# Two stacked blocks on one core: where the head shares, their spreads and the stick weights' meetings stand in a hand-written order

## The chip, the cores and the metric

One core of a Trainium2 chip runs the whole program. The metric is the device time of one execution in microseconds; the kernel before took 3168.99 us, the median of three runs (3164.33 to 3171.9). The engines are named as in the profile: PE is TensorE, DVE VectorE, ACT ScalarE, POOL GpSimd, SP the queue that issues most transfers.

## The reference

A first block of two layers, then a second block of one layer, all float32, on 1024 tokens of width 1024.

```python
def first_block(...):                      # two layers
    for i in range(DEPTH):
        hn = rmsnorm(h, norm1[i])
        z = hn @ w_in[i]
        ...
        pool_out = pool_mixer(u, pool_w[i], pool_scale[i])
        attn_out = dilated_mixer(q, k, v)
        h = h + jnp.concatenate([pool_out, attn_out], axis=-1) @ w_out[i]
        hn = rmsnorm(h, norm2[i])
        h = h + jnp.square(jax.nn.relu(hn @ w_up[i])) @ w_down[i]
        gate = jax.nn.sigmoid(rmsnorm(h, norm3[i]) @ w_gate[i])
        h = h + gate * (p[i] @ w_ple[i])
    return rmsnorm(h, final_norm)
```

The dilated mixer has 12 heads in three groups (patterns) of four. Each group attends in its own windows; a softmax over the three groups' log-sums gives each group a share for every token and head, and the group's output is scaled by it:

```python
    wts = jax.nn.softmax(jnp.stack(lses, axis=0), axis=0)
    o = jnp.concatenate([outs[g] * wts[g][..., None] for g in range(len(DIL_PATTERNS))], axis=2)
```

The second block has eight heads of stick-breaking attention beside a causal convolution of 31 taps:

```python
        causal = s_pos < t_pos
        log_fail = jnp.where(causal, jax.nn.log_sigmoid(-z), 0.0)
        later = lax.cumsum(log_fail, axis=3, reverse=True) - log_fail
        w = jnp.where(causal, jnp.exp(jax.nn.log_sigmoid(z) + later), 0.0)
        outs.append(jnp.einsum('bhts,bshd->bthd', w.astype(vb.dtype), vb))
```

## The kernel before, in words

Every large product is made in three matmuls per piece of the contraction (high and low parts of both operands). A **half** is one output panel of 128 features by 512 tokens: eight **chunks** in the projections (three matmuls of 512 columns each), five in part A of the output product and three in part B. The halves of a layer are numbered m = 2 * panel + token half. Two PSUM banks take the halves of the projections and of parts A and B in turn (`half_bank_no`), so half m + 2 cannot start before DVE has taken half m.

All smaller work is placed between chunks by a table: `weave` (L198) puts jobs at (m, k), that is behind chunk k of half m; `put_a` does the same for part A, counting chunks from its start, five to a half. Each engine goes through the same table. PE does a job's matmuls behind the chunk named. DVE and ACT, however, go through all jobs of half m in the order of k and then take half m (DVE `woven` and `take_qk`, `take_v`, `add_to`; ACT `woven`). So a job's place on DVE is ahead of the take of its half, and a waiting job holds back all behind it.

The jobs at stake in the first block, done for two sets of heads (c = 0 and 1) in each of two layers:

- `step`: attention of one unit (one pattern, two heads). ACT writes each unit's statistics to DRAM (L1891 to L1897), and SP reads the three patterns of a set back (`read_stats`, L878, waited for as `stats_in`).
- `shares`: on DVE `share_weights` (L2352 to L2374) clears `rows` in set 0, waits for the read-back and makes the softmax over groups in eight small steps; ACT gives the exponential (L1915). PE has nothing to do in it.
- `turn_w`: PE turns the weights (L1387) into the one side bank, ACT copies the high part (L1920), DVE makes the low part (L2379, `lower_rows`).
- `spread`: PE spreads a group's rows over its features (L1395) into the side bank, DVE multiplies the attention output by them (L2387), ACT makes the high part (L1924), DVE the low part (L2389); the last two are `weigh`. Each needs the side bank free of the job before it (`side_starts`, L1288).

In set 0 the jobs lie in the halves 28 to 33, eight chunks each, with attention steps of unit 3 between them; in set 1 in part A, halves 48 to 53.

The second block's attention goes over four pairs of heads (c = 0 to 3) and 12 rounds each, placed every fourth chunk as a step u (`weave2`, L330). One step does, on PE, `turn_weights` of round u - 2 (L1615, waits for DVE's product `z_weighed`, L2718), after groups of rounds are complete a `meet` with the values (L1602; groups 0 to 3 at u = 4, 6, 10 and 14, of 8, 16, 24 and 32 matmuls in the profile's count) and `score` of round u (L1628). ACT makes two sigmoids of the scores (L2116, L2117), DVE scans (L2711, L2713) and multiplies (L2718), POOL masks and also splits the weights of the panels (L1168, L1171). The steps 12 to 14 of a pair lie in steps 0 to 2 of the next (`step_parts`). Pair 3 runs in the halves of Z_ATT, where DVE has the gates to take as well.

Of the kernel before, what the change touches and what calls it, by code (L numbers as in the profile page):

```python
# [197 lines left out]
def weave():  # L198
    at = {}

    def put(m, k, *job):
        at.setdefault(m, []).append((k, job))

    def put_a(u, *job):
        put(2 * PART_A + u // len(CHUNKS_A), u % len(CHUNKS_A), *job)

    put(3, 4, "stat", 0)
    put(5, 4, "stat", 1)
    for hf in range(2):
        put(UP_AT[hf], 7, "stat2", hf)  # L210
        put(GATE_AT + 2 * hf, 7, "stat3", hf)
        for c in range(2):
            put(late_at(1 + 2 * hf, c), 2, "turn_p", c, hf)
    for unit in range(UNITS - 1):
        m0 = 2 * (2 + 3 * (unit + 1))
        put(m0, 1, "turn_v", unit, 0)
        put(m0, 4, "turn_v", unit, 1)
        for i in range(STOPS):
            k = 11 + 10 * i
            put(m0 + k // KC, k % KC, "step", unit, i)  # L220
    for c in range(2):
        for hf in range(2):
            put(26 + c, 0 + 4 * hf, "pool", c, hf)
    put(28, 3, "stat_in", 0)
    put(29, 4, "shares", 0)
    for hf in range(2):
        put(30 + 2 * hf, 0, "turn_w", 0, hf)
        put(30 + 2 * hf, 4, "spread", 0, hf, 0)
        put(31 + 2 * hf, 0, "spread", 0, hf, 1)
        put(31 + 2 * hf, 4, "spread", 0, hf, 2)  # L230
    put_a(1, "turn_v", 5, 0)
    put_a(4, "turn_v", 5, 1)
    for i in range(STOPS + LAG):
        put_a(8 + 7 * i, "step", 5, i)
    put_a(36, "stat_in", 1)
    put_a(41, "shares", 1)
    for hf in range(2):
        put_a(45 + 10 * hf, "turn_w", 1, hf)
        for g in range(GROUPS):
            put_a(48 + 10 * hf + 2 * g, "spread", 1, hf, g)  # L240
    for m in at:
        at[m].sort(key=lambda x: x[0])
    return at
# [67 lines left out]
PAIRS = 4  # L311
# [13 lines left out]
ROUNDS = [(qb, part, min(HALF, P * (qb + 1) - HALF * part)) for qb in range(8) for part in range(1 + qb // 4)]  # L325
# [26 lines left out]
def step_parts(c, u):  # L352

    return ((c - 1, u + len(ROUNDS)), (c, u)) if c and u < MEET_LAG else ((c, u),)
# [9 lines left out]
def meets_after(u):  # L364

    r = u - MEET_LAG
    if 0 <= r and ROUNDS[r][0] % 2 and (r + 1 == len(ROUNDS) or ROUNDS[r + 1][0] != ROUNDS[r][0]):
        return ROUNDS[r][0] // 2
    return None
# [38 lines left out]
def two_blocks(nc, x, p, positions, norm1, w_in, pool_w, pool_scale, w_out, norm2, w_up, w_down,  # L408
# [848 lines left out]
    def _(pe):  # L1257
# [332 lines left out]
        def meet(c, g):  # L1590


            group = 4 * c + g
            r = max(i for i, (qb, part, n) in enumerate(ROUNDS) if qb == 2 * g + 1)
            pe.wait_ge(z_taken, 2 * (len(ROUNDS) * c + r + 1))
            if group:
                pe.wait_ge(att_taken, group)
            for kb in range(7, 5 - 2 * g, -1):
                at = max(0, 7 - kb - 2 * g) * P
                for e in range(2):  # L1600
                    rows = slice(64 * e, 64 * e + 64)
                    mm = t.matmul(meet_bank[rows, at:256], v2[c % 2][:, kb, rows], weight_t[:, kb, e, at:256],  # L1602
                                  start=(kb == 7), stop=True, skip_group_check=True)
            mm.then_inc(z_met, 1)

        def turn_weights(c, r):
            nth, blocks = len(ROUNDS) * c + r, ROUNDS[r][2] // P
            pe.wait_ge(z_weighed, nth + 1)
            if r == 0:
                pe.wait_ge(v2_taken, 2 * c + 2)  # L1610
            for e in range(2):
                if nth:
                    pe.wait_ge(z_taken, 2 * (nth - 1) + e + 1)
                for i in range(blocks):
                    mm = t.transpose(turn_banks[e][:, i * P:i * P + P], weight[:, nth % 2, e, i * P:i * P + P], ident[:])  # L1615
                mm.then_inc(z_turned, 1)
# [14 lines left out]
        def woven2(m2, k):  # L1631
            for at, job in WEAVE2.get(m2, ()):
                if at != k:
                    continue
                kind, args = job[0], job[1:]
                if kind == "stat":
                    sum_features(DEPTH, args[0], sum_no(DEPTH - 1, Y_HN1, 7, args[0]) + 1, *job)
                elif kind == "turn_v2":
                    turn_v2(*args)
                else:  # L1640
                    for c, u in step_parts(*args):
                        if TURN_LAG <= u < len(ROUNDS) + TURN_LAG:
                            turn_weights(c, u - TURN_LAG)
                    for c, u in step_parts(*args):
                        if meets_after(u) is not None:
                            meet(c, meets_after(u))
                    for c, u in step_parts(*args):
                        if u < len(ROUNDS):
                            score(c, u)

# [1264 lines left out]
```

## Time and profile before

| | |
|---|---|
| median of 3 runs | 3168.99 us (3164.33, 3168.99, 3171.9) |
| profiled execution, its time | 3167.66 us |
| profiled execution, its span | 3165.9 us |
| PE busy | 3121.7 us, 99% |
| DVE busy | 2045.6 us, 65% |
| POOL busy | 1713.6 us, 54% |
| ACT busy | 977.1 us, 31% |
| granted TensorE clock, mean | 0.996 |

The span runs from the first to the last instruction; the execution's own time has 1.8 us more around it. Busy PE is not PE at its peak: a matmul counts while it runs, at whatever clock was granted. A line of the views reads: start, duration, engine and line of the kernel, what it writes and reads, and in brackets how long the engine had been idle and what released it.

### The profile page before, as it was taken

How to read it: one execution, taken by the hardware profiler on the slowest of the kernel's cores; microseconds unless marked ns; L12 is line 12 of the kernel's file. 1: busy time of each engine (PE TensorE's matmuls, PEld its weight loads, DVE VectorE, ACT ScalarE, POOL GpSimd, SP SyncE). 2: the span in 40 equal slices, each digit the busy share in tenths (PEclk: the TensorE clock that was granted, in tenths of full speed). 3: DMA queues.
4: the chain of work that ended last, by engine and by line, in shares of the span. 5: the costliest groups of instructions: out<-in, count | busy, mean ns of one | idle time of the engine just before them, and what ended most of it. 6: DMA issues, size and time to landing. Idle time of an engine off the chain costs nothing.

```text
span 3165.9 us, 39438 instructions
## 1 busy us (share of the span) xinstructions
PE 3121.7 (99%) x14756; PEld 2518.2 (80%) x14756; DVE 2045.6 (65%) x2749; ACT 977.1 (31%) x1847; POOL 1713.6 (54%) x1544
## 2 busy tenths in 40 slices
PE   8999999999999999999999999999999999999999
PEld 6777788888888888777788888888888776688887
DVE  6656476666665664555676666664768988798323
ACT  3222253333332421222343333332432244402112
POOL 5632355666566546522465666565445533376574
PEclk9999999999999999999999999999999999999999
DMA  5211211111112122112131111112111100011112
GB/s 155 55 40 37 81 57 54 54 52 49 56 54 67 45 94 62 40 41 86 39 57 54 54 48 53 55 54 66 46 47 47 34 27 27 21 50 47 50 54 87
DMA packets 306349, 173.73 MB, mean 55 GB/s; under 512 B 61424, under 2 KB 296944, under 8 KB 306160
## 3 DMA queue, kind: packets, MB, share of 16 engines
q1 hardware_dynamic: 287904, 162.55, 17.7%
q10 hardware_dynamic: 18256, 8.67, 0.9%
q8 instruction: 118, 1.93, 0.2%
q14 instruction: 71, 0.58, 0.1%
HBM read 155.13 MB, written 12.91 MB: 53 GB/s over the span
## 4 chain that ended last, share of the span: by engine, by line
PE 91%; DVE 7%; issue 1%; ACT 1%; DMA 0%; ACTq 0%; DVEq 0%; SPq 0%
PE ring L1261 17%; PE ring L1263 16%; PE ring L1262 16%; PE aux L1261 5%; PE aux L1263 5%; PE aux L1262 5%; PE ring L1523 3%; PE ring L1522 3%; PE ring L1521 3%; PE aux L1523 2%; PE aux L1522 2%; PE aux L1521 2%; DVE conv_out L2670 1%; PE aux L1341 1%; PE aux L1358 1%; PE aux L1602 1%
## 5 line engine op out<-in xcount | busy, mean ns | idle before, releaser
L1010 POOL TENSOR_TENSOR w_hi<-w_raw,ones 128x512 fp32r<-128x512 f32 (+3 forms) x408 | 449.9, 1103 | 894.2 <-PE ring L1263 712.3
L1013 POOL TENSOR_TENSOR w_lo<-w_raw,w_hi 128x512 fp32r<-128x512 f32 (+3 forms) x408 | 533.9, 1308 | 32.0
L1261 PE MATMUL ring<-Q_hi,w_hi 128*128 128x512 f32 x1312 | 519.1, 396 | 0.0
L1263 PE MATMUL ring<-Q_hi,w_lo 128*128 128x512 f32 x1312 | 511.3, 390 | 0.0
L1262 PE MATMUL ring<-Q_lo,w_hi 128*128 128x512 f32 x1312 | 510.9, 389 | 0.0
L1261 PEld LDWEIGHTS ring<-Q_hi,w_hi 128*128 128x128 f32 x1312 | 246.2, 188 | 76.3 <-issue 26.4
L1263 PEld LDWEIGHTS ring<-Q_hi,w_lo 128*128 128x128 f32 x1312 | 246.3, 188 | 52.3
L1262 PEld LDWEIGHTS ring<-Q_lo,w_hi 128*128 128x128 f32 x1312 | 246.4, 188 | 50.4 <-issue 1.0
L1261 PE MATMUL ring<-P_hi,w_hi 128*128 128x512 f32 x656 | 271.0, 413 | 3.0 <-DVE pool_u L2288 1.3
L1262 PE MATMUL ring<-P_lo,w_hi 128*128 128x512 f32 x656 | 258.2, 394 | 0.0
L1263 PE MATMUL ring<-P_hi,w_lo 128*128 128x512 f32 x656 | 258.0, 393 | 0.0
L1261 PE MATMUL aux<-Q_hi,w_hi 128*128 128x512 f32 x544 | 213.2, 392 | 0.0
L1263 PE MATMUL aux<-Q_hi,w_lo 128*128 128x512 f32 x544 | 211.7, 389 | 0.0
L1262 PE MATMUL aux<-Q_lo,w_hi 128*128 128x512 f32 x544 | 211.7, 389 | 0.0
L1974 ACT ACTIVATE aux<-tmp 128x512 f32<-128x512 f32 x112 | 67.4, 602 | 403.2 <-DVE tmp L2435 403.2
L2670 DVE SCALAR_TENSOR_TENSOR conv_out<-conv_in,taps,conv_out 128x1021 f32<-128x1021 f32 (+29 forms) x120 | 185.7, 1594 | 0.2
L1261 PEld LDWEIGHTS ring<-P_hi,w_hi 128*128 128x128 f32 x656 | 124.8, 190 | 42.7 <-issue 14.3
L1263 PEld LDWEIGHTS ring<-P_hi,w_lo 128*128 128x128 f32 x656 | 124.4, 190 | 27.3
L1262 PEld LDWEIGHTS ring<-P_lo,w_hi 128*128 128x128 f32 x656 | 124.6, 190 | 25.9 <-issue 2.9
L1037 POOL TENSOR_TENSOR w_lo<-w_sums,w_hi 128x1024 fp32r<-128x1024 f32 x56 | 134.5, 2401 | 0.0
L1025 POOL TENSOR_TENSOR w_sums<-w_raw 128x256 f32<-128x256 f32 x56 | 41.4, 739 | 159.5 <-issue 152.7
L1261 PEld LDWEIGHTS aux<-Q_hi,w_hi 128*128 128x128 f32 x544 | 102.1, 188 | 22.1 <-DVE Q_lo L2252 0.8
(400 smaller groups left out, 7043.1 us busy)
## 6 DMA issues: line engine op xcount, KB each, us to landing
w_raw<-in_w_in SPq DMA_DIRECT2D x84, 512.0 KB, 3.8
w_raw<-in_w_up SPq DMA_DIRECT2D x64, 512.0 KB, 4.0
w_raw<-in_w_down SPq DMA_DIRECT2D x64, 512.0 KB, 3.4
h_scratch<-h ACTq DMA_DIRECT2D x16, 512.0 KB, 3.7
w_raw<-in_w_gate SPq DMA_DIRECT2D x16, 512.0 KB, 4.0
hx<-h_scratch SPq DMA_DIRECT2D x12, 512.0 KB, 7.8
x_raw<-in_x SPq DMA_DIRECT2D x8, 512.0 KB, 7.7
w_raw<-in_w_out SPq DMA_DIRECT2D x16, 256.0 KB, 2.8
```

Of the source, the lines that this page charges most:

```text
L1010: g.tensor_tensor(w_hi[:, slot, ks], w_raw[:, slot, ks], one.broadcast_to([P, width, P]), ALU.mult).then_inc(w_hi_ready, 1)
L1013: g.tensor_tensor(w_lo[:, slot, ks], w_raw[:, slot, ks], w_hi[:, slot, ks].bitcast(F32), ALU.subtract).then_inc(w_ready, 1)
L1025: g.tensor_tensor(s1, a21, a22, ALU.add).then_inc(s_made, 1)
L1037: g.tensor_tensor(w_lo[:, slot], w_sums[:, slot], w_hi[:, slot].bitcast(F32), ALU.subtract).then_inc(w_ready, 1)
L1261: t.matmul(o, wh, xh, start=first, stop=False)
L1262: t.matmul(o, wh, xl, start=False, stop=False)
L1263: return t.matmul(o, wl, xh, start=False, stop=last)
L1521: t.matmul(to[at], wh, xh, start=(i == 0 and not joins), stop=False, skip_group_check=True)
L1522: t.matmul(to[at], wh, xl, start=False, stop=False, skip_group_check=True)
L1523: mm = t.matmul(to[at], wl, xh, start=False, stop=(i == 1), skip_group_check=True)
L1974: a.activation(square_bank, tmp[:], ACT.Square).then_inc(squared, 1)
L2670: v.scalar_tensor_tensor(conv_out[:, c, shift:], conv_in[:, c, 0:S - shift], tap, conv_out[:, c, shift:], ALU.mult, ALU.add)\
```

## The change

Three edits. In `weave` the job `shares` of set 0 goes from (29, 4) to (28, 6). The turnings and spreads of set 1 go from part A's chunks 45, 48, 50, 52 and 55, 58, 60, 62 to 45, 49, 52, 55 and 59, 63, 66, 69. In PE's `woven2` the meeting of a stick step goes ahead of its turning, except for groups 0 and 1 of the pairs 0 to 2; where a step serves two pairs, all of the earlier pair's work now goes ahead of all of the next one's.

```diff
--- before.py
+++ after.py
@@ -222,7 +222,7 @@
         for hf in range(2):
             put(26 + c, 0 + 4 * hf, "pool", c, hf)
     put(28, 3, "stat_in", 0)
-    put(29, 4, "shares", 0)
+    put(28, 6, "shares", 0)
     for hf in range(2):
         put(30 + 2 * hf, 0, "turn_w", 0, hf)
         put(30 + 2 * hf, 4, "spread", 0, hf, 0)
@@ -235,9 +235,9 @@
     put_a(36, "stat_in", 1)
     put_a(41, "shares", 1)
     for hf in range(2):
-        put_a(45 + 10 * hf, "turn_w", 1, hf)
+        put_a(45 + 14 * hf, "turn_w", 1, hf)
         for g in range(GROUPS):
-            put_a(48 + 10 * hf + 2 * g, "spread", 1, hf, g)
+            put_a(49 + 14 * hf + 3 * g, "spread", 1, hf, g)
     for m in at:
         at[m].sort(key=lambda x: x[0])
     return at
@@ -1639,12 +1639,15 @@
                     turn_v2(*args)
                 else:
                     for c, u in step_parts(*args):
-                        if TURN_LAG <= u < len(ROUNDS) + TURN_LAG:
+                        group = meets_after(u)
+                        turns = TURN_LAG <= u < len(ROUNDS) + TURN_LAG
+                        early = group is not None and group < 2 and c < PAIRS - 1
+                        if turns and early:
                             turn_weights(c, u - TURN_LAG)
-                    for c, u in step_parts(*args):
-                        if meets_after(u) is not None:
-                            meet(c, meets_after(u))
-                    for c, u in step_parts(*args):
+                        if group is not None:
+                            meet(c, group)
+                        if turns and not early:
+                            turn_weights(c, u - TURN_LAG)
                         if u < len(ROUNDS):
                             score(c, u)
 
```

Below the third edit all line numbers are three higher. The order of DVE in layer 0, set 0, from the last attention statistics of half 29 on, before:

```order
L2343 TENSOR_SCALAR neg_max<-row_stat 128x2
L2358 MEMSET rows 128x512
L2360 TENSOR_TENSOR top<-read_back 128x16
L2362 TENSOR_TENSOR top<-top,read_back 128x16
L2364 TENSOR_TENSOR share<-read_back,top 128x48
L2366 TENSOR_TENSOR shared_sum<-share,read_back 128x48
L2368 TENSOR_TENSOR total<-shared_sum 128x16
L2370 TENSOR_TENSOR total<-total,shared_sum 128x16
L2372 RECIPROCAL total<-total 128x16
L2374 TENSOR_TENSOR weights<-share,total 128x48
L2308 TENSOR_TENSOR q_t_82<-ring,rope_c 128x4x128
L2299 TENSOR_TENSOR q_t_82<-q_t_82,swapped_rows 128x4x128
```

And in the changed kernel, from the last operation ahead of half 28's take on (L2361 is L2358 of before, and so on):

```order
L2302 TENSOR_TENSOR k_t_85<-k_t_85,swapped_rows 128x512
L2361 MEMSET rows 128x512
L2363 TENSOR_TENSOR top<-read_back 128x16
L2365 TENSOR_TENSOR top<-top,read_back 128x16
L2367 TENSOR_TENSOR share<-read_back,top 128x48
L2369 TENSOR_TENSOR shared_sum<-share,read_back 128x48
L2371 TENSOR_TENSOR total<-shared_sum 128x16
L2373 TENSOR_TENSOR total<-total,shared_sum 128x16
L2375 RECIPROCAL total<-total 128x16
L2377 TENSOR_TENSOR weights<-share,total 128x48
L2311 TENSOR_TENSOR q_t_82<-ring,rope_c 128x4x128
L2315 TENSOR_TENSOR s_half<-ring,rope_s 128x512
```

The share chain (MEMSET to `weights`) stood behind the attention step of half 29 and ahead of that half's take; it now stands ahead of the take of half 28 (`q_t<-ring,rope_c`), with the step behind it.

PE at step 6 of pair 3, where `ident,weight` is the turning, `weight_t,v` the meeting and `k,q` the score (+ is the changed kernel):

```order
 L1262 MATMUL ring<-Q_lo,w_hi 128x512
 L1263 MATMUL ring<-Q_hi,w_lo 128x512
+L1602 MATMUL aux<-weight_t,v_1_159 64x256 x6
+L1602 MATMUL aux<-weight_t,v_1_159 64x128 x2
 L1615 MATMUL aux<-ident,weight 128x128 x4
 L1615 MATMUL ring<-ident,weight 128x128 x4
-L1602 MATMUL aux<-weight_t,v_1_159 64x256 x6
-L1602 MATMUL aux<-weight_t,v_1_159 64x128 x2
```

The 8 matmuls of the meeting went ahead of the turning; the score stays behind both.

PE in part A of layer 0, behind the first turning of set 1 (`rows,sel` is a spread, the others are chunks of the output product):

```order
 L1262 MATMUL ring<-shared_lo_97,w_hi 128x512
 L1263 MATMUL ring<-shared_hi_95,w_lo 128x512
+L1261 MATMUL ring<-pool_hi,w_hi 128x512
+L1262 MATMUL ring<-pool_lo,w_hi 128x512
+L1263 MATMUL ring<-pool_hi,w_lo 128x512
 L1395 MATMUL ring<-rows,sel 128x512
 L1261 MATMUL ring<-pool_hi,w_hi 128x512
 L1262 MATMUL ring<-pool_lo,w_hi 128x512
 L1263 MATMUL ring<-pool_hi,w_lo 128x512
-L1261 MATMUL ring<-pool_hi,w_hi 128x512
-L1262 MATMUL ring<-pool_lo,w_hi 128x512
-L1263 MATMUL ring<-pool_hi,w_lo 128x512
```

The first spread went one chunk back, the second is two chunks on, outside this piece.

## Rows read from the trace of the kernel before

**Rows 1.** The page, busy time of each engine, its share and instructions.
```profile
PE 3121.7 (99%) x14756; PEld 2518.2 (80%) x14756; DVE 2045.6 (65%) x2749; ACT 977.1 (31%) x1847; POOL 1713.6 (54%) x1544
```

**Rows 2.** Waits of PE, whole span: us in total, times, longest.
```profile
PE ring L1387 <- DVE weights L2374: 8.8, 2, 4.4
...
PE aux L1615 <- DVE weight L2718: 5.6, 4, 2.0
...
PE ring L1395 <- DVE attn L2387: 2.0, 4, 0.5
```

**Rows 3.** Stretches: us, busy time (and instructions) by engine, PEclk, DMA share, GB/s.
```profile
237.22:241.80 4.58, 4.58 (x13) 3.53 (x14) 3.09 (x4) 0.59 (x1) 0.00 (x0) 0.51 0.04 7
...
2704.92:2710.30 5.38, 5.38 (x28) 3.02 (x29) 4.42 (x7) 1.21 (x3) 0.00 (x0) 0.68 0.12 35
```

**Rows 4.** Timeline of PE, halves 30 to 32: start, us, engine, line, operation, [idle <-releaser].
```profile
237.22 1.01 PE L1387 MATMUL ring<-ident,weights 128*6 128x128 f32 x4 [4.40 <-DVE weights L2374]
...
242.50 0.39 PE L1395 MATMUL ring<-rows,sel 128*128 128x512 f32 x1
...
257.26 0.60 PE L1387 MATMUL ring<-ident,weights 128*6 128x128 f32 x4
...
262.52 0.47 PE L1395 MATMUL ring<-rows,sel 128*128 128x512 f32 x1 [1.88 <-DVE rows L2379]
```

**Rows 5.** Timeline of DVE, halves 28 to 30 of layer 0.
```profile
224.62 1.05 DVE L2308 TENSOR_TENSOR q_t<-ring,rope_c 128x512 f32<-128x512 f32 x1 [4.71 <-PE ring L1263]
225.59 0.69 DVE L2312 TENSOR_TENSOR s_half<-ring,rope_s 128x512 f32<-128x512 f32 x1
...
231.04 0.48 DVE L2358 MEMSET rows<- 128x512 f32 x1
...
236.99 1.05 DVE L2308 TENSOR_TENSOR q_t<-ring,rope_c 128x512 f32<-128x512 f32 x1
...
239.66 0.68 DVE L2379 TENSOR_TENSOR rows<-ring,rows 6x512 fp32r<-6x512 f32 x1
```

**Rows 6.** Read-back of statistics, layer 0: the SP queue's timeline, then its landing.
```profile
218.90 0.37 SPq L878 DMA_DIRECT2D read_back<-stats_scratch  x1
...
read_back<-stats_scratch SPq DMA_DIRECT2D x1, 48.0 KB, 4.2
```

**Rows 7.** Timeline of DVE, the share chain of set 1.
```profile
357.95 0.36 DVE L2360 TENSOR_TENSOR top<-read_back 128x16 f32<-128x16 f32 x1
...
361.34 0.21 DVE L2374 TENSOR_TENSOR weights<-share,total 128x48 f32<-128x48 f32 x1
```

**Rows 8.** Timelines of PE and DVE, spreads of set 1.
```profile
368.42 0.50 PE L1395 MATMUL ring<-rows,sel 128*128 128x512 f32 x1 [0.51 <-DVE attn L2387]
...
365.07 0.69 DVE L2387 TENSOR_TENSOR attn<-ring,attn 128x512 f32<-128x512 f32 x1 [1.07 <-PE ring L1395]
...
367.09 0.68 DVE L2545 TENSOR_TENSOR hx<-ring,hx 128x512 f32<-128x512 f32 x1
```

**Rows 9.** Timeline of PE, stick of pair 3.
```profile
2704.92 0.66 PE L1615 MATMUL aux<-ident,weight 128*128 128x128 f32 x4 [2.02 <-DVE weight L2718]
...
2728.15 0.66 PE L1615 MATMUL aux<-ident,weight 128*128 128x128 f32 x4 [1.91 <-DVE weight L2718]
...
2744.78 0.65 PE L1615 MATMUL aux<-ident,weight 128*128 128x128 f32 x4 [0.70 <-DVE weight L2718]
```

**Rows 10.** The chain that ended last: start, us, what.
```profile
2514.45 1.67 PE aux L1602 x16
...
2706.01 3.05 PE aux L1602 x16
```

**Rows 11.** Timeline of DVE, stick of pair 3.
```profile
2711.48 2.50 DVE L2713 TENSOR_TENSOR_SCAN left<-fail,not_yet 128x512 f32<-128x512 f32 x2 [1.79 <-ACT fail L2116]
...
2734.14 2.50 DVE L2713 TENSOR_TENSOR_SCAN left<-fail,not_yet 128x512 f32<-128x512 f32 x2 [0.81 <-ACT fail L2116]
...
2738.60 4.21 DVE L2711 TENSOR_TENSOR_SCAN left<-fail,left 128x511 f32<-128x511 f32 x2 [0.60 <-ACT fail L2116]
```

## The prediction

> **What bounds the kernel now.** The busy times come first: the matmul engine (PE) works 3121.7 of 3165.9 us [rows 1], so only its idle time and the time that it spends at a lower clock can be won, and no edit here removes a matmul. The view of waits then says who holds PE up [rows 2]. Three of its lines touch the change: the turning of the shares waits for the vector engine (DVE), 2 times, 8.8 us in all; the turning of the stick weights waits for DVE, 4 times, 5.6 us; the spreads of the second set wait for the product that reads the side bank before them, 4 times, 2.0 us. That is 16.4 us. The stretches show a second price: after the wait at 237.22 the granted clock is 0.51 for 4.58 us, after the one at 2704.92 it is 0.68 over 5.38 us [rows 3], so part of each runs at 1.2 and not at 2.4 GHz. Last, the engines' own rows give the order at each place [rows 4 to 11].
>
> **Shares of the first set.** PE puts the turning of half 30 behind its first chunk and waits 4.40 us, to 237.22 [rows 4]. DVE is late because its share job stands in the list behind the attention step of half 29: it starts with the clearing of rows at 231.04, and behind it come the take of half 29 at 236.99 and the low rows at 239.66 [rows 5]. The change puts the same nine instructions ahead of the take of half 28. DVE sat idle 4.71 us before that take, from 219.91 to 224.62 [rows 5]; the clearing fits there at no cost. The rest needs the statistics read back. That transfer is issued at 218.90 and takes 4.2 us, so it is there at 223.1 [rows 6]. The chain then costs between 3.60 us, as in the second set (357.95 to 361.55) [rows 7], and some 6 us as here, where it shares its time with GpSimd (231.04 to 236.99) [rows 5]. I take the first, since it is the same chain away from the attention step, and end at 226.7, at most 229.1. Queued behind it is the take of half 28, 1.7 us (224.62, then 225.59 for 0.69) [rows 5]: it ends at 228.4 to 230.8 instead of 226.3. Its bank is wanted by PE at the start of half 30, near 232, so nobody waits; the swaps that the SP queue issues behind this take, and the weight load behind them, go up to some 4 us later, and their readers come a half or more afterwards. The turning, due at 237.22 - 4.40 = 232.82, finds its weights made. What is late next? The spread four chunks on. From the take of half 29 to the end of the low rows DVE needs 3.35 us (236.99 to 240.34) [rows 5]; the take can now start at about 232.2, when its half is done, so they end at 235.6. From turning to spread PE needs 3.38 us at full clock: in the second half 257.26 to 262.52 less the 1.88 us of waiting [rows 4]. The spread is due at 236.2, so no wait comes back. Besides, the 5.28 us from 237.22 to 242.50 [rows 4] shrink to 3.38, which is 1.90 us of clock. Sum per layer 4.40 + 1.90 = 6.30, in two layers **12.6 us**. Upper bound: all that the stretch lost, 4.58 x 0.49 = 2.24, gives 13.3. Lower bound: a wait of 1.88, as the second half of this set has at the same place [rows 4], takes the place of the old one: 12.6 - 3.8 = 8.8.
>
> [...]
>
> **Spreads of the second set.** The third spread of each half waits 0.51 us [rows 8]: two chunks after the one before is too soon. A chunk is about 0.7 us: the 3.38 us above less the turning's 0.60, by four [rows 4]. One more covers the wait: 4 x 0.51 = 2.04 us gained. The last spread now stands behind the end of half 53, and both it and the one before fall into the same DVE list, ahead of the take of that half. A weighing takes DVE 2.02 us (365.07 to 367.09) and the take 0.68 [rows 8]; with the spread's 0.50 this is 3.2 us for one, and about 3.6 when the previous weighing is still in the way, against the next half's five chunks, 3.5 us, until PE wants the bank again. So there may be a new wait per layer, of nothing up to the 0.51 that these spreads waited so far; I take 0.2. Sum **1.6 us**, between 1.0 and 2.0.
>
> **Stick.** In pair 3 every meeting is now ahead of the turning; in the other pairs that of group 2 is, and that of group 3 goes ahead of the next pair's first turning. Of the four waits only one lies in another pair, at a meeting of group 1 whose order stays, so the other pairs give nothing. In pair 3 the turning of step 6 waits 2.02 us and that of step 10 waits 1.91 [rows 9]. The meeting behind them does not need the new weights: 16 matmuls are 1.67 us at full clock, but 3.05 after the 2.02 us wait [rows 10]. Put ahead, it hides 1.67 of 2.02 us, and with 0.35 us idle the clock should hold, so the score comes about 3.4 us earlier. But PE then waits for DVE again: the last turning, step 13, waits 0.70 us already [rows 9]. So PE gains there what DVE gains, and DVE can only lose its own idle time, that spent on scores: 1.79 + 0.81 + 0.60 = 3.20 us [rows 11]. I take **3.2 us**. Bounds: one scan pair more or fewer beside GpSimd, 4.21 against 2.50 us [rows 11], gives 1.5 or 4.9.
>
> **Sum.** 12.6 + 1.6 + 3.2 = 17.4 us. Against the profiled execution (3167.66 us) that gives 3150.3; the median of the runs shown, 3168.99, stands 1.3 us higher, so I forecast **3151.6 us**. With all low bounds 11.3 us (3157.7), with all high ones 20.2 us (3148.8).
>
> **Rivals.**
> - The first set's wait moves to its spread (the low bound above): 8.8 + 1.6 + 3.2 = 13.6, 3155.4 us. For it: DVE shows exactly this in the second half. Against: there a step stands directly before, here none does. 12%.
> - The stick gives nothing: with the scores earlier, GpSimd's weight splits fall on DVE's scans, the wait at step 13 grows above 2 us and the clock falls there, at 5.38 x 0.32 = 1.7 us [rows 3]. 12.6 + 1.6 - 1.7 = 12.5, 3156.5 us. Against: DVE's 3.20 us of idle time are real. 8%.
> - The fall of the clock near 2706 is not due to the wait and stays or moves: 1.7 us less, 15.7, 3153.3 us. For it: waits of 1.88 and 1.91 us have no such fall near them. 4%. [...]
> - Slower: the read-back is late. DVE now waits in order for it ahead of the take of half 28, and PE needs that bank near 232. With chain and take of 5.3 to 7.7 us behind the landing, PE waits once the landing passes 224.3 to 226.7; measured is 223.1 [rows 6]. Each microsecond beyond costs one per layer. To lose 6.3 us net it would have to come 23.7 / 2 = 11.9 us past that point: about 3175 us. 2%.
> - The change does too little to see: the waits return at the next instruction. 3166 us. 4%.
>
> **Numbers.** The forecast as worked out has the remaining 70%. A measurement of this kernel tells apart about 0.2%, 6.3 us; the three runs shown spread over 7.6 us. The range is 3147 to 3158.5: the bounds of the sum, the first three rivals, and 1 to 2 us of scatter; it leaves out the last two rivals. Faster 0.94, same 0.04, slower 0.02.
>
> **What would show it.** The shares' turning has no line among the waits and the granted clock is full after it, in both layers; the share chain on DVE starts near 220 and resumes at the landing; the second half's wait of 1.88 us is still there. The third spreads show no wait; a small one may appear at the start of half 55. In pair 3 step 6 waits about 0.35 us, step 10 nothing, step 13 up to 1.5 us, and the stretch from step 6 to the last meeting is 3 to 4 us shorter. I am wrong if a wait of over 1 us appears before the spread of half 30 or at the start of half 30, or if the stick keeps its length.

## The result, and the profile after

The changed kernel takes **3148.39 us**, median of 4 runs (3147.88 to 3148.72), against 3167.69 us for the kernel before in the same measurement (4 runs, 3164.33 to 3171.9): ratio 0.9935, 95% interval 0.9923 to 0.9947. Forecast were 3151.6 us, with a range of 3147 to 3158.5. The gain is 19.3 us where 17.4 were worked out. Of the 3.2 us between forecast and time, 1.3 are the base: the forecast was counted from 3168.99 us, and the kernel before has 3167.69 here. Timed once more beside the experiments, the changed kernel gave 3148.39 us again (5 runs), and the kernel before 3168.95 (9 runs).

The page of the changed kernel, its busy times, which answer to [rows 1]:

```profile
span 3146.5 us, 39438 instructions
...
PE 3116.4 (99%) x14756; PEld 2515.3 (80%) x14756; DVE 2038.8 (65%) x2749; ACT 978.4 (31%) x1847; POOL 1717.0 (55%) x1544
```

PE is busy for 5.3 us less with the same instructions. Most of that is clock; some of it is only in the counting, since a matmul's row ahead of a wait is counted 0.16 us longer than its place in a steady row (shown under e2). The rest of the gain is idle time.

The view of waits of PE over the whole span, which answers to [rows 2] (columns: waited for, us in total, times, longest):

```profile
PE ring L1395 <- DVE rows L2382: 3.7, 2, 1.9
...
PE aux L1615 <- DVE weight L2721: 2.2, 3, 1.7
...
PE ring L1317 <- DVE v_feat L2324: 0.5, 2, 0.3
```

The lines for the turning of the shares (8.8 us) and for the spreads behind the product that reads the bank (2.0 us) are gone. The stick's line fell from 5.6 to 2.2 us. The second half's wait for the low rows, 1.88 us in each layer, stands as before [rows 4]; it is now the largest that this part of the program has left.

DVE's timeline in the first set of layer 0, which answers to [rows 5]:

```profile
220.19 0.48 DVE L2361 MEMSET rows<- 128x512 f32 x1
222.83 0.85 DVE L2363 TENSOR_TENSOR top<-read_back 128x16 f32<-128x16 f32 x1 [2.16 <-DMA read_back<-stats_scratch]
...
225.40 0.21 DVE L2377 TENSOR_TENSOR weights<-share,total 128x48 f32<-128x48 f32 x1
225.52 1.05 DVE L2311 TENSOR_TENSOR q_t<-ring,rope_c 128x512 f32<-128x512 f32 x1
...
232.40 1.07 DVE L2311 TENSOR_TENSOR q_t<-ring,rope_c 128x512 f32<-128x512 f32 x1 [1.18 <-PE ring L1263]
...
235.12 0.68 DVE L2382 TENSOR_TENSOR rows<-ring,rows 6x512 fp32r<-6x512 f32 x1
```

The clearing runs where the prediction put it, then DVE waits 2.16 us for the read-back, and the chain is over at 225.61, 2.8 us after it resumed. The take of half 28 begins 0.90 us later than before (225.52 against 224.62 [rows 5]; 0.23 of that is the longer start of this execution), that of half 29 waits for PE as it should, and the low rows end at 235.80.

PE's timeline at the same place, which answers to [rows 4]:

```profile
232.88 0.60 PE L1387 MATMUL ring<-ident,weights 128*6 128x128 f32 x4
...
236.07 0.40 PE L1395 MATMUL ring<-rows,sel 128*128 128x512 f32 x1
...
256.08 0.47 PE L1395 MATMUL ring<-rows,sel 128*128 128x512 f32 x1 [1.88 <-DVE rows L2382]
```

No wait stands at the turning or at the first spread. Between the low rows' end (235.80) and the spread (236.07) lie 0.27 us: it was closer than the prediction's 0.6.

The stretches of PE (columns: window, its length, busy time and instructions of PE, PEld, DVE, ACT and POOL, then granted clock, DMA share, GB/s): from the turning to the first spread in both layers, then from the second half's spread to the next in layer 1 and in layer 0:

```profile
232.88:236.07 3.19, 3.19 (x17) 2.62 (x16) 2.88 (x4) 0.59 (x1) 3.11 (x3) 1.00 0.03 8
1391.85:1395.04 3.19, 3.19 (x18) 2.62 (x16) 2.88 (x4) 0.59 (x1) 3.11 (x3) 1.00 0.00 0
...
1415.04:1419.69 4.65, 4.65 (x13) 3.69 (x14) 1.81 (x3) 0.63 (x1) 0.00 (x0) 0.63 0.42 111
256.08:259.12 3.04, 3.04 (x14) 2.52 (x14) 1.80 (x3) 0.63 (x1) 0.00 (x0) 1.00 0.12 22
```

Before, the stretch behind the turning ran at 0.51 of full clock in layer 0 [rows 3] and at 0.52 in layer 1 (1404.65 to 1409.23); both run at the full 2.4 GHz now. The third is new: behind the 1.86 us wait of layer 1 a part of the stretch is at 1.2 GHz, and 1.6 us of the gain are given back there. The same wait in layer 0 has no such fall.

PE's timeline in the stick, pair 3, which answers to [rows 9]:

```profile
2687.81 1.04 PE L1602 MATMUL aux<-weight_t,v 128*64 128x256 f32 x10
2689.08 0.66 PE L1615 MATMUL aux<-ident,weight 128*128 128x128 f32 x4 [0.23 <-DVE weight L2721]
...
2698.27 0.66 PE L1615 MATMUL aux<-ident,weight 128*128 128x128 f32 x4 [0.28 <-DVE weight L2721]
...
2707.58 2.60 PE L1602 MATMUL aux<-weight_t,v 128*64 128x256 f32 x24
2710.29 0.66 PE L1615 MATMUL aux<-ident,weight 128*128 128x128 f32 x4
```

The first row shows the last 10 of the meeting's 16 matmuls. The meeting comes first and the turning waits only 0.23 us at step 6 and next to nothing at step 10; the 0.28 us at 2698.27 is the turning of step 8, which has no meeting beside it. Where the time is bound now is shown by the chain that ended last, from step 10 to step 13 (start, us, what):

```profile
2710.47 1.93 DVE left L2714 x2
...
2719.53 3.92 DVE left L2714 x2
2723.57 1.79 DVE weight L2721
2725.41 0.66 PE aux L1615 x4
```

It runs along DVE's scans and weighings, and PE waits 1.72 us at step 13 (0.70 before [rows 9]). DVE's timeline, at the three places where it had been idle for 1.79, 0.81 and 0.60 us before [rows 11]:

```profile
2693.76 2.54 DVE L2716 TENSOR_TENSOR_SCAN left<-fail,not_yet 128x512 f32<-128x512 f32 x2
...
2715.61 2.33 DVE L2716 TENSOR_TENSOR_SCAN left<-fail,not_yet 128x512 f32<-128x512 f32 x2
...
2719.53 3.91 DVE L2714 TENSOR_TENSOR_SCAN left<-fail,left 128x511 f32<-128x511 f32 x2 [0.23 <-DVE weight L2721]
```

No idle time is left but the 0.23 us behind each weighing, which stood before too. From the scan ahead of step 6 to the end of the last weighing DVE takes 41.91 us where it took 45.44: 3.5 us less, 3.2 of them idle time.

### The span cut at four landmarks

Every kernel below, the experiments' too, can be cut at four starts on PE: the first pooling turn of layer 0, that of layer 1, the first score of the stick and its last meeting. These are lengths in us, each from one profiled execution, worked out from starts in PE's timeline. "Rest" runs to the end of the span.

```
kernel                        start   layer 0  layer 1    stick    rest
before                       201.16   1167.76  1117.13   265.71  414.14
changed                      201.39   1159.27  1110.32   261.40  414.15
changed, once more           201.49   1159.22  1110.40   261.39  414.15
e1 shares only               198.98   1161.10  1110.55   267.70  414.16
e2 spreads only              201.46   1166.31  1114.65   266.53  414.15
e3 meetings only             200.25   1167.13  1116.67   261.39  414.14
e4 meeting first everywhere  202.55   1159.19  1110.29   262.11  414.15
e5 meetings, pair 3 only     200.56   1167.43  1116.60   262.85  414.14
e6 shares at (29, 2)         200.75   1159.52  1108.77   261.39  414.15
e7 late spread               199.29   1158.73  1108.16   261.37  414.15
e8 late end of stick         200.14   1159.19  1110.73   261.59  412.14
e9 e7 and e8                 201.23   1158.96  1108.61   261.60  412.09
e11 e9 and late turns of v   202.07   1157.36  1106.85   261.57  412.08
```

Changed against before: 8.49 in layer 0, 6.81 in layer 1, 4.31 in the stick, less 0.23 in the start and 0.01 in the rest, 19.37 us; the spans differ by 19.4. The start varies by 3.6 us between kernels that are alike in it, so small gains are read from the other columns and not from a single span. The start holds differences that no edit touches: they are not explained here.

### The profile page after: what moved, and what is told of

Its sections match the earlier page's. It is cut to its first block, busy times and chain, and to the rows that moved or that the text cites. A ratio compares the mean times of both kernels' runs of the same rounds, so it can differ in the third digit from the quotient of the medians.

```text
span 3146.5 us, 39438 instructions
## 1 busy us (share of the span) xinstructions
PE 3116.4 (99%) x14756; PEld 2515.3 (80%) x14756; DVE 2038.8 (65%) x2749; ACT 978.4 (31%) x1847; POOL 1717.0 (55%) x1544
## 4 chain that ended last, share of the span: by engine, by line
PE 94%; DVE 4%; issue 1%; ACT 1%; DMA 0%; ACTq 0%; DVEq 0%; SPq 0%
PE ring L1261 17%; PE ring L1263 17%; PE ring L1262 17%; PE aux L1261 5%; PE aux L1263 5%; PE aux L1262 5%; PE ring L1523 3%; PE ring L1521 3%; PE ring L1522 3%; PE aux L1521 2%; PE aux L1523 2%; PE aux L1522 2%; PE aux L1341 1%; PE aux L1358 1%; PE aux L1628 1%; PE aux L1602 1%
```

## The experiments

### Each part alone

**e1_shares**, the kernel before with the first edit only:

```
-    put(29, 4, "shares", 0)
+    put(28, 6, "shares", 0)
```

> Kernel before with one part of the change: the set-0 shares at (28, 6) instead of (29, 4). Theory 1 (the waits at the first spread of set 0 are the price of a share chain that starts too late, in both layers): both waits go, the first spread of layer 0 comes about 6.4 to 6.7 us earlier and that of layer 1 as much again, so 12.6 to 13.3 us off in all, about 3154.5 to 3155.5. The 1.88 us wait of the second half's spread stays in both layers; in the profile of the change it had a clock fall behind it in layer 1 only. If that fall (about 1.6 us) comes here too, the gain reads some 1.6 us smaller. Rival (the gain of the change in set 0 exists only beside the other two edits): under 10 us, with a new wait at or before half 30.

Measured: 3153.09 us median (3150.37 to 3158.54, 4 runs) against 3168.55 (19 runs), ratio 0.9952, interval 0.9937 to 0.9967. Layer 0 is 6.66 us shorter and layer 1 is 6.58, **13.2 us** in all, at the top of what theory 1 expected; the rival is out. (The medians differ by 15.5 us, but this kernel's four runs lie 8.2 us apart, and the columns are one execution each.) No clock fall stands behind the 1.90 us wait of either layer here. The view of waits holds no line for the turning of the shares any more, and the others as they were:

```profile
PE aux L1615 <- DVE weight L2718: 5.6, 5, 2.1
PE ring L1395 <- DVE rows L2379: 3.8, 2, 1.9
PE ring L1395 <- DVE attn L2387: 2.0, 4, 0.5
```

The stick, which this edit does not touch, was 1.99 us longer than in the kernel before. PE's timeline has both long waits of pair 3 in it, and the clock fell behind both, while before it fell only behind the first:

```profile
2689.67 0.66 PE L1615 MATMUL aux<-ident,weight 128*128 128x128 f32 x4 [2.01 <-DVE weight L2718]
...
2713.04 0.66 PE L1615 MATMUL aux<-ident,weight 128*128 128x128 f32 x4 [2.05 <-DVE weight L2718]
```

Its runs lie 8.2 us apart and those of the changed kernel 0.8; that the one comes from the other fits, and was not tried by itself.

**e2_spreads**, the kernel before with the second edit only:

```
-        put_a(45 + 10 * hf, "turn_w", 1, hf)
+        put_a(45 + 14 * hf, "turn_w", 1, hf)
...
-            put_a(48 + 10 * hf + 2 * g, "spread", 1, hf, g)
+            put_a(49 + 14 * hf + 3 * g, "spread", 1, hf, g)
```

> Kernel before with one part of the change: turnings and spreads of set 1 set further apart. The prediction gave this 1.6 us (four waits of 0.51 us less a new one). Theory 1 (a wait costs more than its idle row: the idle is counted from the end of the last matmul, 0.16 us after its place in the steady row, and the restart behind the wait takes about 0.12 us longer): each layer gives about 1.8 us, 3.7 us together, about 3164. Rival (the 1.84 us seen in each layer of the change is owed to the shares having moved, which lets the halves before set 1 end earlier): 1.6 us or less here, about 3166.

Measured: 3164.75 us (10 runs), ratio 0.9984, interval 0.9975 to 0.9994. Layer 0 is 1.45 us shorter although the stretch behind its long wait took 0.18 us more than before (237.49 to 242.95, against 237.22 to 242.50), so the edit gave about **1.6**; layer 1 is 2.48 us shorter, of which 0.74 is clock (1403.54 to 1408.03, 4.49 us, against 5.23), so **1.7**. Together 3.4 us: theory 1, near its number. No new wait came at half 55:

```profile
PE ring L1387 <- DVE weights L2374: 8.8, 2, 4.4
PE aux L1615 <- DVE weight L2718: 5.8, 6, 2.0
PE ring L1395 <- DVE rows L2379: 3.7, 2, 1.9
PE ring L1317 <- DVE v_feat L2321: 0.6, 2, 0.3
```

Why four waits of 0.51 us give 3.4 and not 2.0 is in PE's timeline of the kernel before:

```profile
364.58 0.39 PE L1395 MATMUL ring<-rows,sel 128*128 128x512 f32 x1
...
366.16 0.39 PE L1395 MATMUL ring<-rows,sel 128*128 128x512 f32 x1
...
370.86 0.60 PE L1387 MATMUL ring<-ident,weights 128*6 128x128 f32 x4
```

From the first spread to the second are two chunks and 1.58 us; from the second to the third, at 368.42 [rows 8], again two chunks, but 2.26 us. The difference is 0.68, where the row of the wait says 0.51. A matmul's row is 0.39 long while the next starts 0.23 behind it, and the idle time is counted from the end of that row: 0.16 us of the wait are hidden in it. Behind the wait, three chunks of 0.68 and a spread of 0.22 make 2.27 us, but the turning comes 2.44 us later: the first matmul behind the waiting spread starts 0.34 us after it, the next ones 0.24, where 0.23 is the rule in this piece. So such a wait costs its row plus about 0.33 us: 0.85 each, 3.4 for four.

**e3_meets**, the kernel before with the third edit only:

```
-                        if TURN_LAG <= u < len(ROUNDS) + TURN_LAG:
+                        group = meets_after(u)
+                        turns = TURN_LAG <= u < len(ROUNDS) + TURN_LAG
+                        early = group is not None and group < 2 and c < PAIRS - 1
+                        if turns and early:
                             turn_weights(c, u - TURN_LAG)
-                    for c, u in step_parts(*args):
-                        if meets_after(u) is not None:
-                            meet(c, meets_after(u))
-                    for c, u in step_parts(*args):
+                        if group is not None:
+                            meet(c, group)
+                        if turns and not early:
+                            turn_weights(c, u - TURN_LAG)
```

> Kernel before with one part of the change: the order of meeting, turning and scoring in the stick. Theory 1 (the gain comes from the two long waits of the fourth pair and the clock fall behind the first of them): 3.7 us, about 3164; the clock stretch at 2706 us is gone, and the waits of the fourth pair at its seventh and ninth steps are 0.3 us or less. A further 1.1 us was seen in the first pair of the change, at its step 6. Theory 1a: that is chance of which of two engines reaches a port first, and may or may not be here. Theory 1b: it is an effect of the new order and is here, 4.8 us together. Rival (the shift of the earlier edits decides how the stick falls): 2 us or less.

Measured: 3161.93 us (10 runs), ratio 0.9982, interval 0.9972 to 0.9991. The stick is 261.39 us long, 4.32 less than before. That lies between the 3.7 of theory 1 and the 4.8 of theory 1b; the cut by pairs under e5 tells why. 1.1 us more of the span is that layers 0 and 1 happened to lose less clock behind their 4.40 us waits (turning to spread 4.78 us in both, against 5.28 and 5.23), and 0.9 is the start.

```profile
PE ring L1387 <- DVE weights L2377: 8.8, 2, 4.4
PE ring L1395 <- DVE rows L2382: 3.8, 2, 1.9
PE aux L1615 <- DVE weight L2721: 2.2, 3, 1.7
PE ring L1395 <- DVE attn L2390: 2.0, 4, 0.5
```

### Which part of the new order does it

**e5_pair3_only**, the order of e3 with the turning first at all groups of the first three pairs:

```
-                        early = group is not None and group < 2 and c < PAIRS - 1
+                        early = group is not None and c < PAIRS - 1
```

> The kernel before with the meeting ahead of the turning in the fourth pair only; in the first three the turning stays first at all groups. It is to say what the stick's 0.41 us waits at step 10 (one to three of them in the kernels with the old order, none with the new) and the 0.93 us wait at step 6 are worth. Theory (the fourth pair carries the gain): first score to last meeting is 261.4 us plus 0.5 for each 0.41 wait that is there, so 261.4 to 263; the kernel before had 265.7, and the part kernels with the old order 267.7 and 266.5. The time is 3162 to 3164. Rival (the gain is spread over the pairs): 264 us or more.

Measured: 3164.86 us (10 runs), ratio 0.9990, interval 0.9981 to 1.0; in time this misses the expected 3162 to 3164 by 0.9 us. The stick is 262.85 us, at the end of what the theory allowed, with three of the 0.41 us waits:

```profile
PE aux L1615 <- DVE weight L2721: 3.6, 7, 1.7
```

All three stand at step 10 of pairs 0 to 2 (2531.00, 2594.72, 2658.37), the step of group 2, and cost 1.46 us together, 0.49 each. Such waits were in e1 (two) and e2 (three); in none of the kernels with the new order at group 2 is there one. The kernel before had none of them in its profile either, but one of 0.93 us at step 6 of pair 0, which is in none of the other twelve profiles.

What belongs to which pair is seen when the stick is cut at the first score of each pair, pair 3 running to the last meeting (us, from the same timelines):

```
kernel                       pair 0   pair 1   pair 2   pair 3
before                        59.96    63.11    63.11    79.52
changed                       59.05    63.21    63.21    75.94
e1 shares only                59.55    63.11    63.74    81.31
e2 spreads only               59.50    63.78    63.73    79.53
e3 meetings only              59.03    63.21    63.21    75.96
e4 meeting first everywhere   59.29    63.45    63.45    75.92
e5 meetings, pair 3 only      59.57    63.66    63.71    75.92
```

Pair 3 gives **3.6 us** against the kernel before and e2, and 5.4 against e1, where the clock fell twice. Pair 0 gives 0.9 in the changed kernel because the 0.93 us wait is not there. The step where it stood has its old order in the changed kernel, and e1 and e2, which do not touch the stick, lack the wait as well; so this 0.9 us can't be called a gain of the new order, and what removes the wait is not shown. Pairs 1 and 2 are 0.1 us *longer* than in the kernel before. The meeting ahead of the turning at group 2 thus saves about 0.5 us in a pair that has the 0.41 us wait, and costs 0.1 in one that has none.

**e4_all_first**, the changed kernel without its exception for groups 0 and 1:

```
-                        early = group is not None and group < 2 and c < PAIRS - 1
+                        early = False
```

> The changed kernel without its exception: in the first three pairs too, the meeting comes ahead of the turning at the steps with groups 0 and 1. Every kernel with the new order so far took 261.4 us from the stick's first score to its last meeting, and had no wait at these steps in the first three pairs. Theory 1 (in the first three pairs VectorE's weight is ready before TensorE comes, so which of meeting and turning is first hides nothing; the exception is neutral): 261.4 us within 0.3, time 3148.4 within 0.5. Theory 2 (the turning later by a meeting of 1.7 us at group 1 makes VectorE and ScalarE late for the next step, and the exception avoids that): a wait of 0.3 to 1.5 us at steps 7 or 8 of each of three pairs, 1 to 4 us longer, 3149.5 to 3152.5.

Measured: 3148.87 us (4 runs), ratio 0.9937, interval 0.9922 to 0.9952. The time and the missing waits go with theory 1, but the stick is 262.11 us, 0.7 longer than theory 1's 261.4, where 0.3 was allowed. Neither theory had the reason: against the changed kernel the lag grows by about 0.15 us at exactly the six steps that the exception names, with no wait behind it, and 0.1 us of it comes back by step 10 of the pair, so 0.24 us a pair is left, 0.12 for each step. Why the two orders differ was not tried. The exception is worth 0.7 us.

### How far the shares have to move

**e6_shares_29_2**, the changed kernel with the shares four chunks later:

```
-    put(28, 6, "shares", 0)
+    put(29, 2, "shares", 0)
```

> The changed kernel with the set-0 shares two chunks ahead of where the kernel before had them, at (29, 2) instead of (28, 6). Theory 1 (VectorE runs its work in the order of the program, and the chain of the shares stood behind the taking of half 28 or 29 only because of its place; any place ahead of half 29's own step is early enough): the wait stays away, same time as the change within 0.3 us, about 3148.4. Theory 2 (it is the distance in time that counts, four chunks are 0.9 us): the read-back lands later than in the change, the chain ends about 1 us later and nothing else shifts, again no loss, since the spread had no wait and the chain was ready about 10 us ahead of it. Rival (the chain falls behind the taking of the half, as in the kernel before): the waits of 4.4 us come back, 12 us lost, about 3160.

Measured: 3148.02 us (4 runs), ratio 0.9934, interval 0.9919 to 0.9948: the same time. DVE's timeline shows the clearing and the chain now behind the take of half 28:

```profile
224.21 1.05 DVE L2311 TENSOR_TENSOR q_t<-ring,rope_c 128x512 f32<-128x512 f32 x1 [4.71 <-PE ring L1263]
...
228.14 0.21 DVE L2377 TENSOR_TENSOR weights<-share,total 128x48 f32<-128x48 f32 x1
...
234.48 0.68 DVE L2382 TENSOR_TENSOR rows<-ring,rows 6x512 fp32r<-6x512 f32 x1
```

Two chunks ahead of the old place are enough, since what held the chain was the attention step of half 29, and (29, 2) is in front of it. Theory 2's number was wrong: expected had been that four chunks are 0.9 us; a chunk is three matmuls, 0.68 us, so they are 2.7, and the chain ended 2.7 us later (228.35 against 225.61). The layers are 1159.52 and 1108.77 us long: layer 0 0.25 longer, layer 1 1.55 shorter. In layer 1 the wait of 1.90 us has no clock fall behind it:

```profile
1414.70:1417.77 3.07, 3.07 (x14) 2.52 (x15) 1.80 (x3) 0.63 (x1) 0.00 (x0) 1.00 0.13 23
```

### What was left to gain

**e7_one_late**, the changed kernel with the first spread of the first set's second half three chunks later:

```
-        put(30 + 2 * hf, 4, "spread", 0, hf, 0)
+        put(30 + 2 * hf, 4 + 3 * hf, "spread", 0, hf, 0)
```

> The changed kernel with one more move: the first spread of set 0's second half three chunks later, (32, 7) instead of (32, 4), in both layers; nothing else moves on any other engine. Theory (the 1.88 us wait there ends when VectorE's rows operation comes, which stands behind 2.1 us of the taking of half 31; three chunks of 0.68 us cover it, and the two later spreads keep their distance to VectorE): the wait is 0.2 us or less, each layer ends its set 0 about 2.1 us earlier (1.88 plus 0.16 of modelled matmul end plus the slower restart), 4.2 us in all, and a clock fall has no wait to follow here: about 3144. Rival (the later spreads, now two chunks nearer, wait for the bank or for the attention rows in its place): a new wait of 1 to 1.9 us at the second or third spread or at the turning of v, and 1 us or less gained, about 3148.

Measured: 3144.52 us (4 runs), ratio 0.9923, interval 0.9909 to 0.9936. By the time alone the theory would pass; the profile says otherwise:

```profile
266.84 0.63 PE L1317 MATMUL ring<-ident,v_feat 128*128 128x128 f32 x4 [1.50 <-DVE v_feat L2324]
```

The 1.88 us wait is gone in both layers, but 1.25 us of it are back at the next turning of v (0.25 before). Layer 0 gained 0.54 us and layer 1 gained 2.16, of which 1.6 is the clock fall that no longer has a wait to follow. So the rival held for the idle time, and the clock paid most of the gain. That the move is what keeps the clock up is not shown, since e6 lacks the fall too, with the wait in its place. The columns give 2.7 us; the medians differ by 3.9.

**e8_late_turn**, the changed kernel with the last two steps of pair 3 three chunks later:

```
-            k = 2 + 4 * u
+            k = 2 + 4 * u + (3 if u > 12 else 0)
```

> The changed kernel with the last two steps of the fourth pair in the stick three chunks later (the turning of round 11 and the last meeting). Theory (the 1.72 us wait of that turning is the price of VectorE's two scans and weight, which the round's scores started; chunks put ahead of it cover it, and what reads the attention stands 14 us behind): wait 0.2 us or less, about 1.9 us gained, 3146.5. Rival 1 (the wait only moves: ScalarE's copies, VectorE's last 4 or 5 operations of the pair or the taking of half 46 and 47 come later by three chunks, and TensorE waits for them at panel 24 or at its odd neighbour): 0.3 us or less gained, with a wait of 1.5 us behind the last meeting. Rival 2: slower, 3149 or more, with half 47's taking holding the next panel by over 2 us.

Measured: 3145.22 us (4 runs), ratio 0.9925, interval 0.9909 to 0.9940. The stick with three more chunks in it (2.05 us) is only 0.2 longer, and the rest 2.0 shorter: **1.8 us**, as the theory said. The medians differ by 3.2 us; the remaining 1.4 us is not in the profile's columns behind the start.

**e9_best** is e7 and e8 together, **e10_change** the changed kernel once more.

> Both of the last two edits together on the changed kernel. Theory: they lie in stages that do not touch, so the gains add, 4.2 and 1.9 us, about 3142 to 3142.5. Rival (one of the two gives nothing): 3144 to 3146.5.

> The changed kernel itself once more, on the chip and in the rounds of the last three kernels. Expected 3148.4 us within 0.8 us. What it is to show beside that: whether a clock fall stands behind a wait of 1.88 us in the set-0 spread of layer 1 again (theory of chance: here it may stand in either layer or none, since the same wait in layer 0 had none; theory of cause: it stands in layer 1 again).

Measured: e9 3143.82 us (4 runs), ratio 0.9920, interval 0.9906 to 0.9933. That lies between the theory's 3142 to 3142.5 and the rival's 3144 to 3146.5: the theory's 4.2 and 1.9 missed by the wait that e7 moved. In the profile its layers are 0.31 and 1.71 us shorter than the changed kernel's, and stick and rest 1.86: 3.9 us, against 4.6 by the medians. e10 gave 3148.39, and the clock fall stands in layer 1 again.

**e11_turn_v**, e9 with the two turnings of v behind the first set two chunks later:

```
-        put(m0, 1, "turn_v", unit, 0)
-        put(m0, 4, "turn_v", unit, 1)
+        put(m0, 3 if unit == UNITS - 2 else 1, "turn_v", unit, 0)
+        put(m0, 6 if unit == UNITS - 2 else 4, "turn_v", unit, 1)
```

> The kernel with both later steps (late first spread of the second half, late end of the fourth pair) and one more move: the two turnings of v of the fifth unit, behind set 0, two chunks later in each layer, since a wait of 1.5 us stood there once the wait at the spread was gone. Theory (v's taking on VectorE ends when it ends, whatever TensorE does, and the copies of the turned v are needed a unit later): the wait falls to 0.2 us or less, 1.4 us gained per layer, 2.8 in all, about 3141. Rival (the next operation that waits for VectorE, the taking of half 34 or the step at half 35, takes the wait over): 3143.5 to 3144 with a wait of 1 to 1.5 us behind it.

Measured: **3140.83 us** (3139.95 to 3141.66, 4 runs) against 3167.9 (13 runs), ratio 0.9912, interval 0.9895 to 0.9928. This is the theory's 3141; the rival, a wait at the next operation, is out. The layers are 1.60 and 1.76 us shorter than in e9, and of all the waits that this study named one line remains:

```profile
PE aux L1615 <- DVE weight L2721: 0.7, 3, 0.3
```

It is 7.6 us below the changed kernel, the fastest of all that ran.

## Why the prediction was right

**Shares, 12.6 forecast, 13.2 measured** (e1). The mechanism held in each step: the clearing in DVE's idle time, the read-back by 223, the take of half 28 a microsecond late at no cost, no wait at the first spread. The chain itself took 2.78 us and not 3.60, where the one taken for it (set 1's) ran beside 2.68 us of GpSimd's work and this one beside 0.82. How much that can matter shows the chain of set 0 before: its operations of 128x16 elements took 0.11 and 0.18 us ahead of GpSimd's work (231.44 and 231.58) and 1.27 us beside it (233.43). The term "4.40 + 1.90" was 0.3 us short per layer in two places: the wait's row hides 0.16 us in the modelled end of a matmul, and 3.38 us as the undisturbed way from turning to spread comes from a stretch whose own wait hides as much; undisturbed it is 3.19. The first rival, a new wait at the spread, is out, though by 0.27 us only.

**What the clock gives back.** The prediction left the second half's 1.88 us wait at its row's price. In the changed kernel it cost 1.6 us more in layer 1 (1415.04 to 1419.69, 4.65 us, against 3.04 in layer 0). So the changed kernel gains 6.81 us in layer 1 and 8.49 in layer 0.

**Spreads, 1.6 forecast, 3.4 measured** (e2). This is the term that was mis-sized most. The step "4 x 0.51 = 2.04 us gained" takes the row's idle for the cost of the wait; it is 0.85 each. The new wait of 0.2 at half 55 did not come.

**Stick, 3.2 forecast, 4.3 measured** (e3). For pair 3, which the 3.2 stood for, 3.6 was measured, and the argument holds in each step. The meeting covers the waits at steps 6 and 10 and the clock holds: the score of step 10 comes 4.6 us earlier in its pair. At step 13 PE gives back 1.0, waiting 1.72 us (forecast: up to 1.5). DVE lost its three idle times, 3.20 us, and 0.3 us of work. "The other pairs give nothing" came near by two misses: 0.9 us in pair 0 from a wait that was in the profile of before alone, which is luck, and 0.1 lost in each of pairs 1 and 2. That the new order at group 2 removes waits of 0.41 us the prediction did not see, and could not from a profile that had none.

**The sum.** e1, e2 and e3 give 13.2 + 3.4 + 4.3 = 20.9 us, less 1.6 for the clock fall in layer 1: 19.3, where the columns of the changed kernel show 19.6. By the columns the parts add, and no edit needs another. By the medians they give 15.5 + 3.8 + 6.6 = 25.9 us against 20.2 for the whole (3168.55 less 3148.39); with 3 to 5 us of uncertainty on each that neither confirms the sum nor speaks against it. How much of the 13.2 there is to win also hangs on the execution: with the 4.78 us from turning to spread of e3 and e5 in place of 5.28 and 5.23, each layer of the kernel before would have had 0.5 us less to give.

**How good the number was.** All three terms were low, by 0.6, 1.8 and 1.1 us, and a loss that the prediction did not have, the 1.6 us of clock in layer 1, hid nearly half of that. So the mechanisms were right, and that the total missed by only 1.9 us is in part luck. The measured 3148.39 us lies 0.4 below the sum of all the high bounds (3148.8) and inside the range by the scatter that was added to it.

**Rivals.** That the stick gives nothing, that the read-back is late, and that nothing is seen are all ruled out by rows above. That the clock fall at 2706 is not due to the wait: it is in none of the ten profiles in which pair 3 meets first, and in all three with the old order (before, e1, e2), so that rival is out too.

## What to carry to other kernels

A short wait of the bounding engine can cost more than its row says (here 0.85 us for a row of 0.51); measure it start to start between two like instructions, with and without the wait. When a wait is taken away, look at what the next instruction on the same engine needs: e7 moved 1.25 of 1.88 us one operation down, and only a second move in the table, e11, collected it. And cut two traces at landmarks before explaining a difference in their spans, since a stage that nobody touched can differ by as much as the edit gives.

## What the runs showed beyond that

**The price of a wait is a draw.** Over the 13 profiles, each of the eight waits of 4.40 us has a stretch at 1.2 GHz behind it, but of different length: turning to spread took 4.49, 4.78 (four times), 5.23, 5.28 and 5.46 us, against 3.19 without. All four waits of 2.01 to 2.05 us have one as well. Of the 29 waits between 1.69 and 1.91 us only four have one, each time the same wait, in layer 1: in the changed kernel, in its repetition, in e4 and in e8, but not in the kernel before, e1, e2, e3, e5 or e6, where the same wait stands. None of the waits of 1.5 us in e7 and e9 has. In the start of the program, among other waits, each profile has one of 3.1 to 3.8 us near 55 us, and a fall next to it. What tells the one from the others was not settled: the stretches compared have the same instructions, and only the shares' place or the start differ between e6 and the changed kernel.

**Scatter goes with pair 3's order, not with the longest waits.** The three kernels with pair 3's old order, and so its waits of about 2 us, lie 7.7 to 8.2 us apart over their runs (before 3164.3 to 3172.0, e1, e2), although e1 has no 4.40 us wait left. With the new order it is 3.5 us in e5 and 5.2 in e3, which both have the 4.40 us waits, 1.2 in the changed kernel over nine runs (3147.6 to 3148.8), and 1.7 to 4.0 over four each in e4, e6, e7, e8, e9 and e11. What makes the rest was not tried.

**Two orders of the same matmuls differ.** In e4, turning and meeting exchanged at six steps cost 0.12 us each on balance, with no wait in the profile.
